# A transformer pair on one core: the gates of one token tile scattered by DMA, a new order of the selection, and more row operations in the u loop

## What is computed

```python
best_s, pos = lax.top_k(cand_s, PEER_TOPK)
expert_idx = jnp.take_along_axis(cand_i, pos, axis=-1)
gates = jax.nn.softmax(best_s, axis=-1)
...
u_sel = u_tab[i_blk]
act = jax.nn.gelu(jnp.einsum('td,thkd->thk', h_blk, u_sel))
w = g_blk * act
return jnp.einsum('thk,thkd->td', w, v_tab[i_blk])
```

## Time and profile before

| | |
|---|---|
| median of the runs | 3815.46 us |
| the profiled execution | 3818.46 us, its span 3816.6 us |
| mean granted TensorE clock | 0.932 |
| expert stage, block to block | 36.29 us |
| u loop, first `uv_lo` to the first v product | 2542.05 to 3232.67 us |
| v loop, first to last product | 3232.67 to 3808.2 us |

### The profile page before, as it was taken

One profiled execution on the slowest core, in us unless ns is written; L12 is line 12 of the kernel. 1 busy time (PEld: TensorE's weight loads), 2 busy tenths in 40 slices (PEclk: granted clock), 3 DMA queues, 4 the chain that ended last, 5 costly groups with the idle time before them and its releaser, 6 DMA issues. The chain is left out here.

```text
span 3816.6 us, 46791 instructions
## 1 busy us (share of the span) xinstructions
PE 3387.5 (89%) x16253; PEld 2821.9 (74%) x16253; DVE 2730.8 (72%) x3557; ACT 1932.5 (51%) x2328; POOL 607.7 (16%) x428
## 2 busy tenths in 40 slices
PE   7697745999999999999299977799999987999998
PEld 3485544777777777777188856589999987777776
DVE  8316536999999999999544226337888766788887
ACT  1225414777777777777124334225878874332332
POOL 0000011001011011010200000000000254555652
PEclk9898867999999999999589978899999998999999
DMA  7520107999999999999633301134545689999997
GB/s 296 176 67 2 46 30 260 375 379 374 378 375 374 378 375 373 379 374 363 239 97 92 98 22 45 63 139 160 183 177 216 258 331 363 358 371 379 385 381 274
DMA packets 217467, 954.88 MB, mean 250 GB/s; under 512 B 23344, under 2 KB 85040, under 8 KB 142448
## 3 DMA queue, kind: packets, MB, share of 16 engines
q1 hardware_dynamic: 161872, 734.91, 52.0%
q0 software_dynamic: 46816, 167.80, 11.7%
q10 hardware_dynamic: 8640, 50.34, 3.2%
HBM read 864.92 MB, written 88.05 MB: 250 GB/s over the span
## 5 line engine op out<-in xcount | busy, mean ns | idle before, releaser
L1394 DVE TENSOR_TENSOR w_low<-w_raw,w_high 128x2048 fp32r<-128x2048 f32 x399 | 908.6, 2288 | 91.3 <-ACT w_high L1323 86.4
L1323 ACT ACTIVATE w_high<-w_raw 128x2048 fp32r<-128x2048 f32 x399 | 765.0, 1917 | 329.9 <-PE ps L125 182.3
L123 PE MATMUL ps<-w_high,xT_high 128*128 128x512 f32 x1056 | 433.6, 411 | 21.8 <-issue 21.8
L2462 DVE TENSOR_TENSOR uv_lo<-uv_raw,uv_hi 128x2048 fp32r<-128x2048 f32 x128 | 293.3, 2292 | 198.8 <-ACT uv_hi L2267 198.0
L124 PE MATMUL ps<-w_low,xT_high 128*128 128x512 f32 x1056 | 418.4, 396 | 0.0
L125 PE MATMUL ps<-w_high,xT_low 128*128 128x512 f32 x1056 | 418.1, 396 | 0.0
L123 PE MATMUL ps<-h4T_high,uv_hi 128*128 128x384 f32 x1024 | 355.9, 348 | 18.5 <-ACT a_out L2304 14.9
L123 PE MATMUL ps<-uv_hi,w_hi 128*128 128x512 f32 x768 | 306.3, 399 | 45.7 <-DVE w_lo L2477 34.8
L124 PE MATMUL ps<-h4T_low,uv_hi 128*128 128x384 f32 x1024 | 346.5, 338 | 0.0
L125 PE MATMUL ps<-h4T_high,uv_lo 128*128 128x384 f32 x1024 | 346.4, 338 | 0.0
L2267 ACT ACTIVATE uv_hi<-uv_raw 128x2048 fp32r<-128x2048 f32 x128 | 244.7, 1912 | 149.0 <-PE ps L125 119.2
(11 more groups left out here) (515 smaller groups left out, 6991.0 us busy)
## 6 DMA issues: line engine op xcount, KB each, us to landing
w_raw<-in_w_gate_up SPq DMA_DIRECT2D x267, 1024.0 KB, 6.9
w_raw<-in_w_down SPq DMA_DIRECT2D x132, 1024.0 KB, 6.9
uv_raw<-in_peer_u SPq DMA_DIRECT2D x64, 1024.0 KB, 5.3
uv_raw<-in_peer_v SPq DMA_DIRECT2D x64, 1024.0 KB, 9.3
wbuf_ada<-in_w_ada SPq DMA_DIRECT2D x12, 2048.0 KB, 8.8
a_rows<-a_out SPq DMA_DIRECT2D x128, 192.0 KB, 2.0
g_rows<-spread ACTq DMA_DIRECT2D x12, 2048.0 KB, 8.4
qT<-g_rows SPq DMA_DIRECT2D x16, 1536.0 KB, 15.1
```

Source lines behind the costliest of these rows:

```text
L123: pe.matmul(out, l_hi, r_hi, start=first, stop=False)
L1323: act.activation(w_hi[:, n % SPLIT, :], w_raw[:, n % RAW, :], ACT.Copy).then_inc(s_wh, 1)
L1394: dve.tensor_tensor(w_lo[:, n % SPLIT, :], w_raw[:, n % RAW, :], w_hi[:, n % SPLIT, :].bitcast(F32), ALU.subtract).then_inc(s_wl, 1)
L2462: dve.tensor_tensor(uv_lo[:, n % 2, :], uv_raw[:, n % 2, :], uv_hi[:, n % 2, :].bitcast(F32), ALU.subtract).then_inc(s_lo, 1)
```

## The change

One of the three dense tiles, tile 1, no longer goes through rounds. Its 128 gates a token are added, by 128 indirect accumulating DMAs of Pool with 128 words each, into `g_scat`, an HBM array of 8.4 MB that a new Pool DMA fills with zeros in the query stage before. The wait of each 16th scatter is for all before it. The selection runs in the order 0, 2, 1, 3, with the sparse tile first. Rounds fall from 96 to 64, stores from 12 to 8. Of tile 3's one-hot rows VectorE makes two instead of one. Row operations in the u loop rise from 74 to 112: one in each of steps 12 to 44 (four in step 22) and four in each of steps 45 to 63. The gate load of the v loop is split in two, as is the product `weights`. In the expert stage a tensor of 432 words a partition, `room_xT`, that nothing uses is put ahead of `xT`.

```diff
     xe = sb(stage, "xe", [P, D])
+    sb(stage, "room_xT", [P, 432])
     xT_hi, xT_lo = (sb(stage, f"xT_{x}", [P, 2, 4 * P], F32R) for x in ("high", "low"))
...
-    ORDER, SPARSE = (1, 2, 0, 3), 2
+    ORDER, SPARSE, SCATTERED = (0, 2, 1, 3), 0, 2
+    HOT = (1, 3)
-    HALVES, RN = DENSE // HALF, HALF // 4
+    HALVES, RN = len(HOT) * P // HALF, HALF // 4
     g_rows = nc.dram_tensor("g_rows", [HALVES, P, PK * HALF], F32, kind="Internal").ap()
+    g_scat = nc.dram_tensor("g_scat", [P, PK * P], F32, kind="Internal").ap()
...
+    def keep_and_zero(pool, s_h):
+        pool.memset(zeros[:, :], 0.0).then_inc(s_zm, 1)
+        pool.wait_ge(s_zm, 1)
+        pool.dma_start(g_scat.rearrange("p (a n) -> p a n", n=2 * D),
+                       zeros[:, :].unsqueeze(1).to_broadcast([P, PK * P // (2 * D), 2 * D])).then_inc(s_zg, 16)
+        pool_steps.on(pool)
+        pool.wait_ge(s_h, 1)
+        pool_steps(pool.tensor_copy(h4_s[:, :], h4[:, 0, :]))
+        pool.wait_ge(s_zg, 16)
...
     MIDDLE = [keys_flat[:, b * D:(b + 1) * D] for b in range(2)] + [work[:, b * D:(b + 1) * D] for b in range(2)]
     LATE = [rows_c[:, 0, :]]
...
-    turns_at = {x: [at + k for k in range(11)] for x, at in enumerate((0, 12, 24, 35))}
-    hots_in = [[1] + [2] * 15 + [1], [2, 2, 2, 1] * 4 + [2, 2], [2, 3] * 6 + [2]]
-    hots_from = (11, 28, 46)
-    rows_in = {45: 2, 46: 4} | {n: 4 for n in range(47, NG)} | {NG + k: 3 if k % 9 else 2 for k in range(NG - 1)}
+    turns_at = {x: [at + k for k in range(11)] for x, at in enumerate((0, 11, 23, 34))}
+    hots_in = [[1, 1, 2] * 7 + [2, 2], [2, 2, 3] * 4 + [2, 2]]
+    hots_from = (22, 45)
+    rows_in = {n: 1 for n in range(12, 45)} | {n: 4 for n in range(45, NG)} | {22: 4}
...
+    work_step = [n for n in range(2 * NG) for kind, x, c in plan[n] if kind == "S" for _ in range(c)]
+    gather_step = []
+    for g in range(2 * SEL):
+        n = work_step[before_of[g]] if before_of[g] >= 0 else max(turns_at[SPARSE]) + 1
+        if g >= MIDDLE_AT:
+            n = max(n, max(turns_at[TT - 1]) + 1)
+        gather_step.append(max(n, gather_step[-1] if g else 0))
+        assert gather_step[g] <= work_step[g]
+    gathers_at = [[g for g in range(2 * SEL) if gather_step[g] == n] for n in range(2 * NG)]
+    scatter_from = max(turns_at[SCATTERED]) + 1
+    MINE = ((0, 1, 2), (0, 1))
+    hots_act, hots_dve = [0], [0]
+    for r in range(len(HOT) * P // 4):
+        n = len(MINE[4 * r // P])
+        hots_act.append(hots_act[-1] + n)
+        hots_dve.append(hots_dve[-1] + 4 - n + 1)
...
+            g_words = g_scat.rearrange("p (n o) -> (p n) o", o=1)
+
+            def scatter(k):
+                if k == 0:
+                    pool.wait_ge(s_sel, SCATTERED + 1)
+                elif k % PT16 == 0:
+                    pool.wait_ge(s_scat, 16 * k)
+                pool.indirect_dma_start(g_words, bass.IndirectOffsetOnAxis(ap=scat_id[:, k:k + 1], axis=0),
+                                        scat_gate[:, k:k + 1], None, compute_op=ALU.add).then_inc(s_scat, 16)
+
+            def gather(g):
+                if g == 0:
+                    pool.wait_ge(s_xr, 16)
+                    pool.wait_ge(s_sel, SPARSE + 1)
...
+            for n in range(2 * NG):
+                for k in range((n - scatter_from) * SCATTERS, (n - scatter_from + 1) * SCATTERS):
+                    if 0 <= k < SEL:
+                        scatter(k)
+                for g in gathers_at[n]:
+                    gather(g)
...
+                    sp.wait_ge(s_scat, 16 * SEL)
-                    sp.dma_start(g_in[:, q % 2, :].rearrange("p (h x) -> p h x", h=HALVES),
+                    sp.dma_start(g_in[:, q % 2, 0:G_HOT].rearrange("p (h x) -> p h x", h=HALVES),
                                  g_rows.rearrange("h p x -> p h x")[:, :, q * GKEYS * HALF:(q + 1) * GKEYS * HALF])\
+                      .then_inc(s_gin[q % 2], 16)
+                    sp.dma_start(g_in[:, q % 2, G_HOT:G_IN], g_scat[:, q * GKEYS * P:(q + 1) * GKEYS * P])\
                       .then_inc(s_gin[q % 2], 16)
...
-                for q in range(3):
+                for q in MINE[tile]:
...
+                if x == SCATTERED:
+                    gates = scat_gate[:, :].rearrange("p (h k) -> p h k", h=PH)
+                    dve.wait_ge(s_col, 1)
+                    st(dve.scalar_tensor_tensor(out=part_f[:, :, :], in0=sel[:, 0, :, :], scalar=float(PK), in1=sel[:, 1, :, :],
+                                                op0=ALU.mult, op1=ALU.add))
+                    st(dve.tensor_scalar(part_f[:, :, :], part_f[:, :, :], float(P), column, ALU.mult, ALU.add))
+                    st(dve.tensor_copy(scat_id[:, :], part_f[:, :, :].rearrange("p h k -> p (h k)")))
...
-                dve.tensor_scalar(first_hot[:, s, 3, :], iota_row[:, :], selT[:, tile % 2, 0, at + 3:at + 4],
-                                  selT[:, tile % 2, 2, at + 3:at + 4], ALU.is_equal, ALU.mult).then_inc(s_hot, 1)
+                for q in range(len(MINE[tile]), 4):
+                    dve.tensor_scalar(first_hot[:, s, q, :], iota_row[:, :], selT[:, tile % 2, 0, at + q:at + q + 1],
+                                      selT[:, tile % 2, 2, at + q:at + q + 1], ALU.is_equal, ALU.mult).then_inc(s_hot, 1)
...
-                gates = g_in[:, q % 2, :].rearrange("p (h j n) -> p j h n", h=HALVES, j=GKEYS)[:, key:key + GROUP, :, :]
-                dve.tensor_tensor(wf[:, :, :].rearrange("p j (h n) -> p j h n", n=HALF),
-                                  a_in[:, p % 2, :, :].rearrange("p j (h n) -> p j h n", n=HALF), gates, ALU.mult).then_inc(s_wf, 1)
+                hot = g_in[:, q % 2, 0:G_HOT].rearrange("p (h j n) -> p j h n", h=HALVES, j=GKEYS)[:, key:key + GROUP, :, :]
+                scattered = g_in[:, q % 2, G_HOT:G_IN].rearrange("p (j n) -> p j n", j=GKEYS)[:, key:key + GROUP, :]
+                dve.tensor_tensor(wf[:, :, 0:P], a_in[:, p % 2, :, 0:P], scattered, ALU.mult).then_inc(s_wf, 1)
+                dve.tensor_tensor(wf[:, :, P:DENSE].rearrange("p j (h n) -> p j h n", n=HALF),
+                                  a_in[:, p % 2, :, P:DENSE].rearrange("p j (h n) -> p j h n", n=HALF), hot, ALU.mult).then_inc(s_wf, 1)
```

More of the change, by code:

```diff
@@ L779, in _ @@
             def _(pool):
-                pool_steps.on(pool)
-                pool.wait_ge(s_h, 1)
-                pool_steps(pool.tensor_copy(keep[:, :], hh[:, 0, :]))
+                keep(pool, s_h)
         @block.scalar
@@ L2010, in emit @@
     h4 = sb(stage, "h4", [P, TT, D])
+    zeros = sb(stage, "zeros", [P, 2 * D])
+    s_zm, s_zg = sem("zeros_here"), sem("gates_zeroed")
+    def keep_and_zero(pool, s_h):
[7 more added lines that the diff above has]
+        pool.wait_ge(s_zg, 16)
     gemm = Gemm(stage, "query", [(4, CH, lambda n: t["peer_w_query_2"][n, :, :])])
@@ L2015, in emit @@
                    copy_out(gemm, nc.scalar, lambda g, i, m: qT4[:, ds(i * 4 + m, 1), :].rearrange("p a n -> p (a n)")), False,
-                   first_loads, h4_s)
+                   first_loads, keep_and_zero)
     stage.close()
@@ L2037, in emit @@
     row_dot = sb(stage, "row_dot", [P, SEL])
-    row_w = sb(stage, "row_w", [P, SEL])
+    scat_id = sb(stage, "scat_id", [P, SEL], I32)
+    scat_gate = sb(stage, "scat_gate", [P, SEL])
+    row_w = scat_gate
+    column = small[:, 40:41]
     psum_g = small[:, 32:40]
@@ L2041, in emit @@
     GKEYS = 8
-    G_IN, A_IN = HALVES * GKEYS * HALF, GROUP * DENSE
+    G_HOT = HALVES * GKEYS * HALF
+    G_IN, A_IN = G_HOT + GKEYS * P, GROUP * DENSE
     assert 2 * (G_IN + A_IN) <= 2 * PH * SEQ
@@ L2065, in emit @@
         sem(f"peer_{x}") for x in ("weights", "weights_high", "weights_low", "outputs", "added", "stored", "x_back"))
+    s_col, s_scat = sem("column"), sem("gates_scattered")
     s_rd, s_rg = sem("rows_used"), sem("rows_gelu")
@@ L2071, in emit @@
     LATE = [rows_c[:, 0, :]]
-    MIDDLE_AT, LATE_AT = 8, 84
+    MIDDLE_AT, LATE_AT = 42, 122
     homes = EARLY + MIDDLE + LATE
@@ L2083, in emit @@
     UNITS_T, UNIT_EXP = 21, 14
-    turns_at = {x: [at + k for k in range(11)] for x, at in enumerate((0, 12, 24, 35))}
-    hots_in = [[1] + [2] * 15 + [1], [2, 2, 2, 1] * 4 + [2, 2], [2, 3] * 6 + [2]]
-    hots_from = (11, 28, 46)
-    rows_in = {45: 2, 46: 4} | {n: 4 for n in range(47, NG)} | {NG + k: 3 if k % 9 else 2 for k in range(NG - 1)}
+    turns_at = {x: [at + k for k in range(11)] for x, at in enumerate((0, 11, 23, 34))}
+    hots_in = [[1, 1, 2] * 7 + [2, 2], [2, 2, 3] * 4 + [2, 2]]
+    hots_from = (22, 45)
+    rows_in = {n: 1 for n in range(12, 45)} | {n: 4 for n in range(45, NG)} | {22: 4}
+    rows_in |= {NG + k: 3 if k % 3 == 0 else 2 for k in range(NG - 1)}
+    SCATTERS = 7
     plan, count, at = [[] for _ in range(2 * NG)], [0] * TT, 0
@@ L2093, in emit @@
             count[x] += c
-    for tile in range(TT - 1):
+    for tile in range(len(HOT)):
         assert sum(hots_in[tile]) == P // 4
@@ L2113, in emit @@
                 count[x] += c
```

(35 more changed lines are left out.)

2 lines of the change are left out of this document (1 added, 1 removed).

## The result

The changed kernel takes 3844.68 us, the median of four runs (3836.65 to 3847.78), beside 3817.72 us for the kernel before in the same series (3813.46 to 3820.96). The ratio is 1.0068, with a 95% interval of 1.0049 to 1.0087: slower by 27 us. The forecast was 3772 us and faster, with a range of 3722 to 3836, so the measured time lies outside the range as well.

What follows compares the result with a forecast made beforehand. TensorE was taken to bound the expert stage, DMA close behind, and DMA the v loop; -26 - 30 + 61 - 17 - 35 + 4 = -43 us on the median 3815.5 gave 3772 us, range 3722 to 3836.

Steps and rivals of the forecast that it cites:

- The unused tensor: Expert stage: room_xT brings products closer together, saving 0.8 us in each of 33 blocks; -26 us, between 0 and -33.
- Pool's queue, steps 34 to 53: Second half of u loop: 169 scatters and gathers at 1.50 us plus waits delay VectorE's rows; +61 us in steps 45 to 52.
- scatters further apart than 1.9 us: Sign in Pool's timeline that would show the forecast wrong; the forecast itself took 1.50 us each.
- Rival 3: Pool's scatters go one at a time, each waiting for its landing, 2.1 us instead of 1.50: 3848 us, slower; 17%.
- Steps 0 to 44: First part of u loop: fewer rounds and stores, 417 us against 446.7, 6 of it for single full steps; -30 us.
- The cover by VectorE: Steps 34 to 44: VectorE's 106.7 us of work fits within TensorE's 109.4, so row operations add no time.
- Steps 53 to 63 and the seam: End of u loop to v loop: less store traffic and one-hot work, 129 us against 145.8; -17 us, bounds 0 and -25.
- The v loop: Gathers fall from 173 to 135, DMA's need drops below the floor, 540 us; -35 us, bounds -26 and -53.
- the floor of 522: v loop: 64 steps that wait for nothing, at 8.16 us each, give 522 us as its least time.
- The zeros: Query stage: filling 8.4 MB with zeros shares the DMA engines and delays TensorE's start; +4 us, between 0 and +22.

## Why the prediction was wrong, by its steps

**The unused tensor** (-26): right, -27 us. The reading of one stage against the others held: with the remainder gone the pace is 0.227 us, and the runs with 48 and 16 words leave the remainder, or something that goes with it, as the cause.

**Pool's queue, steps 34 to 53** (+61): this is the step that failed, a term mis-sized. The queue was the right place, and a late row did hold up `row_work`, the next `low` and TensorE. But the forecast had 1.50 us for each of 169 instructions, from the gathers. The windows of Pool's two lines in the changed kernel show from 2831.46 to 3180.00 (length, then busy and count):

```profile
2831.46:3180.00 348.54, 236.80 (x126) 0.83 0.63 178
...
2831.46:3180.00 348.54, 42.39 (x42) 0.83 0.63 178
```

With 0.30 of issue a scatter takes 2.18 us and a gather 1.31. So against the forecast it is +86 for the scatters, -8 for the gathers and +13 for the waits (20 us, not 7): some 350 us of queue instead of 261. Of these 89 us, 46 appear in steps 45 to 52 and 16 to 19 in the steps behind them; the rest found cover. The plain scatters have a mean of 1.32 us, 1.62 with the issue, and with them steps 45 to 52 fell to 154 us: near the forecast's price of 1.50 the forecast's 159 us nearly came out. One of the signs that were named for being wrong, scatters further apart than 1.9 us, was met by their mean of 2.18.

No row of the kernel before showed what the addition costs Pool: the plain scatter of the routing stage takes 0.96 us there, about as long as a gather. And I had let the upper bound be a gather's longest cadence. An operation that no row shows deserved a wider one: 0.40 us more was enough to turn the sign, and it was 0.68.

**Rival 3** (3848 us) gave nearly the measured time by another mechanism. Scatters don't wait for each other's landing: their starts are 1.86 us apart, while the chain of waits shows 3.27 us from the start of the last of 16, at 2955.32, to its landing, and 9.40 us at 2906.95. What is long is Pool's own instruction. This is what speaks against the rival; the plain scatters alone would not, since without the addition it would have forecast a shorter time as well.

The Trainium skill ("DMA: Bandwidth & Descriptors", section "Anatomy of one DMA — SWDGE (gpsimd) path") puts most of its fixed 2.0 us into completion. The traces fit that: plain scatters follow each other by 1.26 us, so what comes behind Pool's instruction overlaps with the next one. The size alone would have made this rival look proved.

**Steps 0 to 44** (-30): -20. Steps 0 to 10 took 88.8 us, as reckoned (88.3). Steps 11 to 33 took 221.0 instead of 212.8, and 34 to 44 took 116.9 instead of 109.4; of the 16 us, the forecast had allowed 6 for single full steps. The cover by VectorE was too thin: it was busy 307.5 of 337.9 us there. Scatters had no part in steps 11 to 33, which take 221.0 us without any as well. With the scattered tile first, which has none of the 25 row operations of these steps there, they take 210.8 us. So the row operations cost about 10 us, 0.4 each, instead of nothing.

**Steps 53 to 63 and the seam** (-17): +7. Without lateness it is 134 to 137 us (3026.3 to 3163.42 without scatters, 3026.2 to 3160.24 with early ones), 5 to 8 above the 129 forecast; why is not shown. The other 16 to 19 are Pool's lateness, which went on past step 52, to the last scatter at 3184.3.

**The v loop** (-35): -38.7, right in size. Its working is borne out in part. The loop took 575 us with 173 gathers (two kernels), 556 and 560 with 161, and 532 and 535 with 149, but 530 to 537 with 135, in five kernels. So it stops 8 to 15 us above the floor of 522, and it is there with 149 gathers already: the last 14 gathers taken out of it bought nothing.

**The zeros** (+4): about nothing. Expert stage and zeros gave -27.1 together, and 33 blocks of 0.82 us are 27.1. With the unused tensor alone, and no zeros, the first `uv_lo` stands at 2513.62, 1.4 us before that of the changed kernel, and two of its variants with the zeros have it earlier still (2511.89 and 2512.86). ScalarE's two waits for the query weights came to 5.6 us instead of 2.6.

## What to carry to other kernels

A queue that serves two customers in program order has a budget: add up its instructions over the stretch between two fixed points and compare with the stretch's length, before asking what each costs. Above the budget the order helps little (seven or five a step: 15 us of 142 that the scatters cost); below it the same work is close to free (the scattered tile first). And an operation that no row of the trace shows must not be priced by a cousin that lacks its special part, here the addition; its bounds should reach as far as the sign of the forecast can turn.

## What the runs showed of the hardware

- An accumulating indirect DMA of 128 words keeps Pool busy for 1.54 us at least, a plain one for 0.95, and a gather of 128 rows of 4 KB for 0.94. Each has 0.30 us of issue.
- Pool's time depends on what VectorE does at that moment. Of the 128 scatters of the changed kernel, the 48 during which VectorE ran no `TENSOR_TENSOR` or `SCALAR_TENSOR_TENSOR` took 1.54 to 1.58 us; the 80 others took 1.55 to 3.72, with a median of 1.90. The scatter at 2846.15 began beside a `uv_lo`, which has two SBUF operands, and took 3.31 us; the next ones ran beside `MAX8`, `FIND_INDEX8` and `MATCH_REPLACE8` and took 1.55.

```profile
2846.15 3.31 POOL L2174 DMA_INDIRECT g_scat<-scat_gate,scat_id  x1 [0.30 <-issue]
2849.76 1.55 POOL L2174 DMA_INDIRECT g_scat<-scat_gate,scat_id  x1 [0.30 <-issue]
```

```profile
2845.71 2.29 DVE L2527 TENSOR_TENSOR uv_lo<-uv_raw,uv_hi 128x2048 fp32r<-128x2048 f32 x1 [4.55 <-ACT uv_hi L2326]
2847.92 0.89 DVE L2410 MAX8 top_s<-ps 128x8 f32<-128x128 f32 x4
```

  3.31 - 1.55 = 1.76 us, and the `uv_lo` ended 1.85 us after the scatter began. The Trainium skill ("SBUF — State Buffer", section "Who interferes with whom") says that a VectorE instruction with two SBUF inputs contends with GpSimd's reads, and that one with a single input, outside the two-port modes, does not. The numbers above agree. The section also infers that a `tensor_tensor` would not hold up the making of descriptors; these scatters were held up beside one, so here the measurement decides.
- Products of 512 float32r columns follow each other by 0.227 us, at full granted clock, where the distance between moving and stationary operand, from the sizes declared, is a multiple of 512 bytes, and by 0.233 to 0.234 us where 320 or 384 bytes are left over. In this kernel 192 unused bytes a partition are worth some 26 us.
